# Two transformer blocks in split fp32: operands moved to 128-byte lines, one key tile, a halved Fourier product, moving averages on another engine

## The reference, cut to what matters

```python
h = rms_norm(x, g_mix) * (1 + scale) + shift      # the same for the context
q, k, v, u_pool, u_four = split(h @ w_in)         # 8 query heads, 2 key/value heads, head width 64
k, q = rope(head_rms(k)), rope(head_rms(q))       # the context's q and k without rope
attn = softmax(q @ concat(k_ctx, k).T / 8) @ concat(v_ctx, v)   # 4 query heads to one key head
pool = (moving_mean(u_pool, windows 2, 4, 8, 16) - u_pool) @ w_pool * pool_scale
four = real(fft2(u_four, positions and the 64 channels of a group)) @ w_four
x = x + gate1 * (concat(attn, pool, four) @ w_out)
x = x + gate2 * (silu(h2 @ w_gate) * (h2 @ w_up)) @ w_down      # h2: x normalised again; width 2816
```

## Time and profile before

| | us |
|---|---|
| median of three runs | 3325.37 (3323.67 to 3326.33) |
| the profiled execution | 3326.27 |
| its span | 3324.4 |
| PE busy in it | 3178.4 |
| granted TensorE clock, mean | 0.99 of full |

### The profile page before, as it was taken

The page is one execution under the profiler, slowest core; times in us unless marked ns, Lnnn a source line. Parts: engine busy times, 40 slices in busy tenths (PEclk is TensorE's granted clock), DMA queues, the critical chain, the costliest instruction groups (busy, mean ns, idle before and its releaser), DMA issues. The chain is left out here.

```text
span 3324.4 us, 51811 instructions
## 1 busy us (share of the span) xinstructions
PE 3178.4 (96%) x21168; PEld 2513.8 (76%) x21168; DVE 1488.4 (45%) x2338; ACT 1177.2 (35%) x1928; POOL 1484.9 (45%) x808
## 2 busy tenths in 40 slices
PE   8899999999999999999999989999999998999999
PEld 6785686888678757867876756888888875678787
DVE  7642294999575324859986244300100023520000
ACT  6225334322352434252225444322122243532221
POOL 4433553544353245344543285344233434745454
PEclk9999999999999999999999999999999998999999
DMA  3012132565220122235542101111121111022222
GB/s 133 9 35 70 45 114 78 205 208 181 75 64 4 48 75 76 90 130 200 202 160 100 45 20 34 56 64 64 51 70 64 64 61 45 20 83 95 95 95 95
DMA packets 77707, 284.44 MB, mean 86 GB/s; under 512 B 8736, under 2 KB 8736, under 8 KB 76960
## 3 DMA queue, kind: packets, MB, share of 16 engines
q1 hardware_dynamic: 77472, 281.13, 25.3%
HBM read 278.99 MB, written 2.10 MB: 85 GB/s over the span
## 5 line engine op out<-in xcount | busy, mean ns | idle before, releaser
L131 POOL TENSOR_TENSOR lows<-ring,highs 128x1024 fp32r<-128x1024 f32 x376 | 944.5, 2513 | 1512.4 <-ACT highs L123 1478.0
L155 PE MATMUL ps<-x_high,highs 128*128 128x512 f32 x2080 | 829.4, 399 | 34.6 <-ACT highs L123 16.8
L158 PE MATMUL ps<-x_low,highs 128*128 128x512 f32 x2080 | 815.4, 392 | 0.0
L123 ACT ACTIVATE highs<-ring 128x1024 fp32r<-128x1024 f32 x376 | 397.0, 1056 | 714.7 <-PE ps L155 369.0
L155 PEld LDWEIGHTS ps<-x_high,highs 128*128 128x128 f32 x2080 | 393.0, 189 | 140.2 <-issue 44.6
L158 PEld LDWEIGHTS ps<-x_low,highs 128*128 128x128 f32 x2080 | 393.1, 189 | 83.3 <-issue 3.8
L1789 DVE CUSTOM_DVE_ANT_0 BR<-BR 128x1024 f32<-128x1024 f32 x144 | 290.8, 2019 | 6.8
L2829 DVE TENSOR_TENSOR hidden_scratch<-ps,hidden_scratch 128x512 f32<-128x512 f32 x44 | 30.5, 692 | 547.0 <-PE ps L2139 538.3
L724 PE MATMUL ps<-x_high,lows 128*128 128x512 f32 x1024 | 252.9, 389 | 0.0
L724 PEld LDWEIGHTS ps<-x_high,lows 128*128 128x128 f32 x1024 | 192.2, 188 | 39.9
L2705 DVE SCALAR_TENSOR_TENSOR BR<-ps,mod,BR 128x512 f32<-128x512 f32 x72 | 47.4, 662 | 367.3 <-PE ps L167 367.3
(11 more groups left out here) (443 smaller groups left out, 5502.5 us busy)
## 6 DMA issues: line engine op xcount, KB each, us to landing
ring<-in_w SPq DMA_DIRECT2D x414, 512.0 KB, 3.5
BR<-in_ada SPq DMA_DIRECT2D x72, 512.0 KB, 3.6
merging<-in_ada SPq DMA_DIRECT2D x24, 512.0 KB, 3.6
X<-in_xT SPq DMA_DIRECT2D x4, 512.0 KB, 6.7
X<-in_memT SPq DMA_DIRECT2D x2, 1024.0 KB, 5.8
BR<-in_cond SPq DMA_DIRECT2D x4, 512.0 KB, 4.5
out<-BR SPq DMA_DIRECT2D x8, 256.0 KB, 4.5
cst<-in_cst SPq DMA_DIRECT2D x1, 1408.0 KB, 6.7
```

Of the source, the lines that this page charges most:

```text
L123: nc.scalar.activation(self.high(n), self.chunk(n), ACT.Copy).then_inc(self.hi_made, 1)
L131: nc.gpsimd.tensor_tensor(self.low(n), self.chunk(n), self.high(n).bitcast(F32), ALU.subtract).then_inc(self.lo_made, 1)
L155: mm = nc.tensor.matmul(ps, high, xhigh, start=start, stop=False)
L158: nc.tensor.matmul(ps, high, xlow, start=False, stop=False)
```

## The change: what it does

- `mods` is allocated ahead of the ring, the context tiles ahead of `cst2`, and `pad` fills up to the next multiple of 128 bytes ahead of `X`, ahead of `mixed` and at the top ahead of `merged`. The square sums (`stats`) move into scratch tensors.
- Query head p and p + 4 share a query tile, so that one key tile with key head 0 in partitions 0 to 63 and key head 1 in 64 to 127 serves all; the columns of `w_in` and the rows of `w_out` are permuted on the way in. The in-projection has 10 tiles for 11, and the hand-written places of the norms move with it.
- The long Fourier product uses the symmetry of cosine and sine: the product with the cosine is made for outputs 0 to n/2, that with the sine for 1 to n/2 - 1, in two PSUM banks. ACT evicts the even part, and DVE writes the upper half in reversed order (even minus odd) and then adds the odd part to the lower half. The tables are two chunks for four.
- In layer 0 the context's moving averages are made by DVE, with scratch of its own, beside x's on POOL.

```diff
+        mods = sb("mods", [P, LAYERS, 96])
+        pad(nc, ctx, "pad", 128, 4 * LAYERS * 96)
         WR = (sb("ring", [P, RING, CW]), sb("highs", [P, PARTS, CW], F32R), sb("lows", [P, PARTS, CW], F32R),
               arrived, used, hi_made, lo_made)
-        mods = sb("mods", [P, LAYERS, 96])
...
+LINE = 128
+
+
+def pad(nc, ctx, name, *sizes):
+
+    used = sum(-(-n // 32) * 32 for n in sizes)
+    if used % LINE:
+        ctx.enter_context(nc.sbuf_tensor(name, [P, (-used % LINE) // 4], F32))
...
+    pad(nc, ctx, "first_pad", 4 * NCST, 4 * NPAR, 64, 4 * RW_TILES, 16, 16 * NCH, 8 * T)
...
+        kept.enter_context(nc.sbuf_tensor(f"top_pad{layer}", [P, 24], F32, side="right"))
...
-STAGE_CHUNKS2 = (("early", EARLY), ("in", 11), ("dft", 4), ("out", 8), ("up0", 2 * FH), ("down0", FH), ("up1", 2 * FH), ("down1", FH))
+STAGE_CHUNKS2 = (("early", EARLY), ("in", 10), ("dft", 2), ("out", 8), ("up0", 2 * FH), ("down0", FH), ("up1", 2 * FH), ("down1", FH))
...
+    HC, HCL = sb("context_high", [P, DK, CTX], F32R)[:, :, :], sb("context_low", [P, DK, CTX], F32R)[:, :, :]
     cst = sb("cst2", [P, NCST2])
     par = sb("par2", [P, NPAR2])
     mod = sb("mod", [P, 48, 2])
     gain = sb("gain", [P, 2, 8, 2])
-    HC, HCL = sb("context_high", [P, DK, CTX], F32R)[:, :, :], sb("context_low", [P, DK, CTX], F32R)[:, :, :]
     xT = BR[:, 8:16, :]
     cT = BR[:, 0:4, :].rearrange("p a t -> p (a t)").rearrange("p (k t) -> p k t", k=DK)
     quarter = BR[:, 4:8, :].rearrange("p a t -> p (a t)")
     spare = sb("spare", [P, 2])
-    stats = {"x": sb("x_squares", [P, T]), "c": sb("context_squares", [P, CTX])}
+    pad(nc, ctx, "second_pad", 4 * NCST2, 4 * NPAR2, 384, 128, 8)
...
-        QR, KR, FO, VV = XT(0, 4), XT(4, 2), XT(13, 2), XT(16, 6, P)
-        QRc, KRc, FOc = XT(6, 4, CTX), XT(8, 2, CTX), XT(15, 2, CTX)
+        QR, KR, FO, VV = XT(0, 4), XT(4, 1)[:, None, :], XT(13, 2), XT(16, 6, P)
+        QRc, KRc, FOc = XT(6, 4, CTX), XT(8)[:, None, 0:CTX], XT(15, 2, CTX)
...
-        tiles = [("q", i) for i in range(4)] + [("k", i) for i in range(2)] + [("v", 0)] + [("p", i) for i in range(2)] + [("f", i) for i in range(2)]
+        tiles = [("q", i) for i in range(4)] + [("k", 0), ("v", 0)] + [("p", i) for i in range(2)] + [("f", i) for i in range(2)]
...
-        KA = XT(18, 2, CKV)
+        KA = Y[:, 18 * T:18 * T + CKV]
...
-        items += [(KR[:, i, :], "k_gain", KA[:, i, CTX:CKV], XT(4 + i)) for i in range(2)]
-        items += [(KRc, "k_gain", KA[:, :, 0:CTX], XT(8))]
+        items += [(KR[:, 0, :], "k_gain", KA[:, CTX:CKV], XT(4)), (KRc[:, 0, :], "k_gain", KA[:, 0:CTX], XT(8)[:, 0:CTX])]
         if update:
             items += [(QRc[:, 2 * i:2 * i + 2, :], "q_gain", QNc[:, 2 * i:2 * i + 2, :], XT(6 + i)) for i in range(2)]
-        turning = 6
-        groups = ((0, 4), (4, min(8, len(items))), (8, len(items)))
+        turning = 5
...
-                        sums(groups[0])
+                        sums((0, 4))
+                    if j == 6:
+                        sums((4, len(items)))
                     if j == 7:
-                        sums(groups[1])
+                        value_turns()
                     if j == 8:
-                        sums(groups[2])
-                        value_turns()
+                        turns(0, 4)
                     if j == 9:
-                        turns(0, 4)
-                    if j == 10:
                         turns(4, turning)
...
                     if j == 3:
                         for i in range(4):
                             act.wait_ge(S("evictedx"), i + 1)
                         squares(0, 4)
                     if j == 4:
-                        logarithms(groups[0])
+                        logarithms((0, 4))
+                        act.wait_ge(S("evictedx"), 5)
+                        act.wait_ge(S("evictedc"), 5 if update else 1)
+                        squares(4, len(items))
                     if j == 5:
-                        act.wait_ge(S("evictedx"), 6)
-                        act.wait_ge(S("evictedc"), 6 if update else 2)
-                        squares(4, len(items))
+                        logarithms((4, len(items)))
                     if j == 6:
-                        logarithms(groups[1])
-                    if j == 7:
-                        logarithms(groups[2])
                         act.wait_ge(S("value_turned"), 1)
                         nc.scalar.activation(VV[:, 2:6, :], PS[:, 3, :].rearrange("p (q c) -> p q c", c=P), ACT.Copy).then_inc(S("value_out"), 1)
                         act.wait_ge(S("value_turned"), 2)
                         nc.scalar.activation(VV[:, 0:2, :], PS[:, 6, 0:CTX].rearrange("p (q c) -> p q c", c=P), ACT.Copy).then_inc(S("value_out"), 1)
-                    if j == (7 if update else 6):
+                    if j == (6 if update else 5):
...
-            return stream.chunk(nd + q).rearrange("p (x t) -> p x t", x=2)[:, x, 0:T:T // n]
+            a, step = q % 2 * T, T // n
+            return stream.chunk(nd + q // 2)[:, a + 256 + step:a + T:step] if x else stream.chunk(nd + q // 2)[:, a:a + 257:step]
...
+            def pooling(eng, g, s, room):
+                u, n, step, done = U[s["name"]], s["n"], S("pool_step" + s["name"]), [0]
+                w = n + 16
+                s2, s4, s8, mean = (room[:, i * XB:i * XB + w] for i in range(4))
+
+                def link(ins):
+
+                    done[0] += 1
+                    ins.then_inc(step, 1)
+                    eng.wait_ge(step, done[0])
+
+                link(g.memset(u["p"][:, :, 0:8], 0.0))
+                link(g.memset(u["p"][:, :, 8 + n:16 + n], 0.0))
+                for c in range(2):
+                    src = u["p"][:, c, :]
+                    link(g.tensor_tensor(s2[:, 1:w], src[:, 0:w - 1], src[:, 1:w], ALU.add))
+                    link(g.tensor_tensor(s4[:, 2:w - 2], s2[:, 1:w - 3], s2[:, 3:w - 1], ALU.add))
+                    lo, hi = s2[0:64, 8:8 + n], s4[64:128, 8:8 + n]
+                    if c:
+                        link(g.tensor_tensor(s8[:, 4:w - 4], s4[:, 2:w - 6], s4[:, 6:w - 2], ALU.add))
+                        link(g.tensor_tensor(s2[64:128, 8:8 + n], s8[64:128, 4:4 + n], s8[64:128, 12:12 + n], ALU.add))
+                        lo, hi = s8[0:64, 8:8 + n], s2[64:128, 8:8 + n]
+                    link(g.tensor_tensor(mean[0:64, 0:n], lo, u["cnt"][0:64, c, :], ALU.mult))
+                    link(g.tensor_tensor(mean[64:128, 0:n], hi, u["cnt"][64:128, c, :], ALU.mult))
+
+                    link(g.tensor_tensor(src[:, 8:8 + n], mean[:, 0:n], src[:, 8:8 + n], ALU.subtract))
+                g.memset(mean[:, 0:1], 0.0).then_inc(S("d" + s["name"]), 1)
 
             @block.gpsimd
             def _(pool):
+                pooling(pool, nc.gpsimd, full[0], Y)
...
-                                mm = nc.tensor.matmul(PS[:, b + c, 0:n], gg[:, q, c, x, :], table(q, x, n), start=(q == 0 and x == 0), stop=(q == nq - 1 and x == 1))
-                                if s is full[-1 if q < 2 else 0] and c == 0 and x == 0:
+                                part = PS[:, b + 2 + c, 0:n // 2 - 1] if x else PS[:, b + c, 0:n // 2 + 1]
+                                mm = nc.tensor.matmul(part, gg[:, q, c, x, :], table(q, x, n), start=(q == 0), stop=(q == nq - 1))
+                                if s is full[-1 if q < 2 else 0] and q % 2 == 0 and c == 0 and x == 0:
...
+            @block.vector
+            def _(dve):
+                if update:
+                    pooling(dve, nc.vector, full[1], mixed)
+                for s in full[::-1]:
+                    nm, n, b = s["name"], s["n"], s["bank"]
+                    for c in range(2):
+                        dve.wait_ge(S("even" + nm), c + 1)
+                        h, f2, odd = n // 2, U[nm]["f2"][:, c, :], PS[:, b + 2 + c, 0:n // 2 - 1]
+                        nc.vector.scalar_tensor_tensor(out=f2[:, n - 1:h:-1], in0=odd, scalar=-U[nm]["norm"], in1=f2[:, 1:h], op0=ALU.mult, op1=ALU.add).then_inc(S("upper" + nm), 1)
+                        dve.wait_ge(S("upper" + nm), c + 1)
+                        nc.vector.scalar_tensor_tensor(out=f2[:, 1:h], in0=odd, scalar=U[nm]["norm"], in1=f2[:, 1:h], op0=ALU.mult, op1=ALU.add).then_inc(S("f_out" + nm), 1)
...
-                        a.activation(U[nm]["f2"][:, c, :], PS[:, b + c, 0:n], ACT.Copy, scale=U[nm]["norm"]).then_inc(S("f_out" + nm), 1)
+                        a.activation(U[nm]["f2"][:, c, 0:n // 2 + 1], PS[:, b + c, 0:n // 2 + 1], ACT.Copy, scale=U[nm]["norm"]).then_inc(S("even" + nm), 1)
...
-            return Pair(lambda u: QN[64 * u:64 * u + 64, p, q * P:(q + 1) * P], lambda u: KA[64 * u:64 * u + 64, p // 2, :],
-                        lambda u, kb: VV[:, kb, (p // 2) * 64:(p // 2) * 64 + 64], CKV,
+            return Pair(lambda u: QN[64 * u:64 * u + 64, p, q * P:(q + 1) * P], lambda u: KA[64 * u:64 * u + 64, :],
```

(23 more changed lines are left out.)

60 lines of the change are left out of this document (18 added, 42 removed).

## The result

The kernel after takes 3292.57 us (median of 4 runs, 3284.92 to 3295.39) against 3324.94 (4 runs, 3323.67 to 3326.33): ratio 0.9899, 95% interval 0.9881 to 0.9916. The forecast was 3285. In the profiled executions 3326.3 became 3291.4 us, a gain of 34.9 where 40.6 was forecast. The sum is near, but some of its terms are not. The spans are 3324.4 and 3289.6 us, and their difference splits as follows.

A forecast was written before the change was run, and what follows sets the result against it. PE, busy for 96% of the span, was taken as the bound. Alignment 10.1, key tile 16.8 + 4.3 and mixing stages 9.4 sum to 40.6 us off 3326.3; with the median 0.9 lower, 3285, range 3265 to 3297.

The forecast's parts named there:

- Alignment, second block: Second block's hidden and mixed matmuls gain from tiles on multiples of 128 bytes: 5.4 us in layer 1, 1.3 in layer 0.
- rivals 3 and 4: Rival 3: alignment unit is 256 bytes, 3266 us, chance 0.13. Rival 4: moved weights slow x matmuls, 3343 us, chance 0.04.
- rival 4: Moving highs and lows 768 bytes against x_high slows x_high and x_low matmuls to 234.2 ns: 3343 us, chance 0.04.
- branches, 1.0 us, and merged, 2.4 us: First block's aligned tiles speed PE: 0.5 us a layer in the merges, 2.4 us in both output stages.
- In the merge, PE waiting for DVE: Sign named for the forecast: in the first block's merges PE would wait for DVE; no size given.
- One key tile: Second block's in-projections: one tile fewer saves 16.8 us, fewer head sums and rotation swaps 4.3, about 10.5 in each layer.
- Halves, layer 1: Layer 1's mixing stage, Fourier product by halves: 5.9 us saved, with the stage ending at the pool products.
- The reversed write: DVE's reversed-order write in the Fourier part: taken to cost nothing, though it might double the time.
- Layer 0's contention, 4.9 us: Layer 0's mixing: DVE's pools hold up POOL by 3.9 us, so 3.5 us are saved instead of 8.4.
- Rival 1: Layer 0's mixing: DVE's pools do not hold POOL up, the other 4.9 us come, 3280 us; chance 0.14.
- The clock of the attention stages: Lower granted clock in layer 1's attention could make the result up to 5 us better or worse; 0 in the sum.

The follow-up runs named there:

- e1: Kernel after with its alignment undone in both blocks, context tiles back on a multiple of 256 bytes: 3296.3 us, ratio 0.9899 to before.
- e0: Kernel after, unchanged, measured again: 3288.6 us, ratio 0.9883 to before.
- e11: Kernel after without first-block alignment, second block's context tiles moved 64 bytes, plus a tail of matmul runs at varied operand offsets of some 100 us: 3389.6 us.
- e7: Kernel after with ada reductions over 256 columns instead of 1024 (work left out) and first block not aligned: 3279.0 us, ratio 0.9850 to before.
- e2: Kernel after with the first block's tiles 96 bytes past a multiple of 128 again, second block aligned: 3285.3 us, ratio 0.9870 to before.
- e5: Kernel before with the one key tile alone, without alignment, Fourier halves and averages on DVE: 3304.8 us, ratio 0.9940 to before.

## Why the prediction was right, and where its steps were wrong

- **Alignment, second block.** Right in size (6.7 forecast; output and feed-forward stages 7.7 us shorter, e1 against after and e0 5.5 to 7.5; in layer 1 these stages take 426.2 us in e1 against 421.0 and 421.2, 5.1 us for 5.4). hidden_parts matmuls now run at the rate of x: over 38 of them in layer 1, 3258.36 - 3249.75 = 8.61 us, 226.6 ns each (rows below). Its reason was wrong: not a multiple of 128 counts, but the distance from the weights. In the kernel before, highs starts 128 bytes past a multiple of 256, hidden_parts 32 and branches_high 96: 160 and 224 bytes apart, which have 234.3 and 232.8 ns in the tail of e11, as the 234.2 and 233 of the earlier trace rows. The context half of hidden_parts was 160 apart too, 117.2 ns in the earlier trace rows and 117.3 in the tail. The pads help because they put these tiles, as x_high already was, at the weights' place modulo 256; they ask for 128 only, and it came out so. That also settles rivals 3 and 4. There is a unit of 256 bytes, but at 0 apart it gives 256 columns no 113.3 ns. And distance does matter, but highs and lows moved by 768 bytes, three whole units, so x_high lost nothing. The argument against rival 4, that the distance changes by 512 or 1536 bytes from one k to the next and the rate does not, could not tell: these too are whole units.

```profile
3249.75 0.39 PE L166 MATMUL ps<-hidden_parts,highs 128*128 128x512 f32 x1
...
3258.36 0.39 PE L163 MATMUL ps<-hidden_parts,highs 128*128 128x512 f32 x1
```

- **branches, 1.0 us, and merged, 2.4 us: the failed step.** I read 0.5 us of DVE waiting for PE and both at 98% as two engines of the same length. Against e7, where PE sets the pace at the same offsets, DVE was 3.8 us longer. DVE has few waits in its list because its waiting for POOL stands inside its operations (1.22 us become 3.3), where no wait list shows it. A faster PE gains nothing there. In place of the 0.5 us a layer forecast as gain the merge ended 1.1 us later: 41 reductions are held up instead of 40, and their sum grows by 3.7 us, in both layers and in after and e0 alike, while e2, which lacks this alignment alone, has the numbers of before. That it comes from the splits starting at other moments is argued; the moment alone was not varied. The output stage gives back what its matmuls save, by 2.17 us of PE waiting for merged_low. "In the merge, PE waiting for DVE" came true, but as a loss. Together 4.6 us lost for 3.4 gained.
- **One key tile.** Right: 10.6 and 10.5 us where 10.5 each were forecast; e5 has it alone, with 10.6 and 12.1, of which 1.6 are put to the clock.
- **Halves, layer 1.** Right: 6.1 us for 5.9. The reversed write costs nothing (255 columns 0.42 us both ways), the even copy 0.39. The stage now ends with POOL, flag at +14.7.
- **Layer 0's contention, 4.9 us: mis-sized.** It came to 0.5. I had POOL's operations grow by 0.42 us each for DVE's turn, from two engines that alternate; they grew by 0.08. There the waiting is DVE's: 11 of its 12 operations are 0.7 to 0.95 us longer than the first, and each ends about 0.2 us into POOL's next one. Rival 1 (8.4 us saved, POOL not held up) was the nearer one, at 7.9. The Trainium skill, "SBUF — State Buffer", "SBUF: two separate sides", has the lock; the trace agrees that there is one, and shows that with the two engines in turn it is here DVE, with the shorter operations, that pays: 0.44 to 1.2 us against 1.06 to 1.14 for POOL. By the line rule of the same page ("Specifications (TRN2)") no offset here should cost anything; 234.3 against 226.7 ns at 160 bytes shows that another rule holds beside it.
- **The rest.** 3.9 us of this one profile (start, between the first block's layers, and behind the block) are not in e0. They came from no edit, and where they arose was not settled. The clock may have a part: from 95 to 110 us of the span it was granted at 0.77 in after and at 0.89 in before and e0. Later runs of after lie at 3286 to 3291, the first four at 3285 to 3295. The clock of the attention stages, put at 0 within 5 us, came out at 0.3 us for both together.

So 40.6 forecast, less 7.2 for merges and output stages in this profile, less 3.9 that no edit explains, plus 4.4 for layer 0's mixing and 0.9 in small items is 34.8: two errors of opposite sign, and the near hit is partly luck.

## What to carry to other kernels

Where two engines show the same busy share, take work from one and see: an engine's busy time can hold its waiting for a third (77 us of DVE's here), and then making the other faster can cost time. Put the moving operand of rounded fp32 matmuls of 512 columns at the weights' place modulo 256 bytes, and do so where PE is really the bound: e2, aligned in the second block alone, is the fastest version that computes everything, at 3285.3 us (0.9870), though its interval overlaps with that of after (0.9883). Two edits on one stage (halves, pools) are to be priced together: the move of the pools was worth 0 without the halves and 3.4 us with them.

## What was not expected of the hardware

- The rate of a 512-column fp32r matmul depends on the distance between weights and moving tile: 226.7 ns at 0, 231.3 at 16, 228.8 at 64, 233 to 234 elsewhere; at 256 columns 113.3 at 64, 114.5 at 192 (117.6 for another pair at this distance), 119 at 0. The place that is best for 512 columns is among the worst for 256.
- A DVE reduction of 1024 columns lasts 1.22 us or, behind a POOL split, 3.3; the same split takes 1.22 us on DVE and 2.3 to 2.4 on POOL.
